# State-space output pass of a two-block model: products one step ahead, decays and outputs in two buffers, skip term on another engine

## What is computed

```python
decay = exp(where(lower, ac[..., :, None] - ac[..., None, :], -inf))       # ac: cumulated log decays of a chunk
y_intra = (einsum(cc, bc) * decay) @ xc                                      # within a chunk
y_inter = (cc * exp(ac)[..., None]) @ s_start                                # from the state at the chunk's start
y = y_f + flip_t(y_b) + d_skip[:, None] * xs                                 # both directions, and the skip term
y = y.reshape(b, T, SSD_DIM) * silu(z)
return rms_norm(y, norm_g)
```

## Time and profile before

| What | Value |
|---|---|
| Median of 3 runs | 3827.31 us (3821.52 to 3830.05) |
| The profiled execution's own time | 3822.47 us |
| Its span | 3820.6 us |
| Busy in the span: TensorE, VectorE, ScalarE, GpSimd | 3531.8, 2709.2, 869.0, 590.5 us |
| `ssd_stage` in it | 2789.6 to 2883.6 us |
| Granted TensorE clock, mean | 0.97 of full speed |

### The profile page before, as it was taken

One profiled execution on the slowest core, in us unless ns is written; L12 is line 12 of the kernel. 1 busy time (PEld: TensorE's weight loads), 2 busy tenths in 40 slices (PEclk: granted clock), 3 DMA queues, 4 the chain that ended last, 5 costly groups with the idle time before them and its releaser, 6 DMA issues. The chain is left out here.

```text
span 3820.6 us, 63639 instructions
## 1 busy us (share of the span) xinstructions
PE 3531.8 (92%) x25982; PEld 2197.3 (58%) x25982; DVE 2709.2 (71%) x3565; ACT 869.0 (23%) x1732; POOL 590.5 (15%) x579
## 2 busy tenths in 40 slices
PE   6999899988889999999999998999976998869995
PEld 2444488874355555555555555644555888435553
DVE  6889599995876676666666763787275778467773
ACT  2000022220122221212212211422235443012322
POOL 1112100004000000000000000321042875000110
PEclk9999999999999999999999999999998999979998
DMA  7674322225689999999999996312003000238996
GB/s 294 238 264 156 141 99 111 110 79 204 253 308 355 329 330 333 323 335 329 331 332 323 331 324 204 127 58 89 33 1 126 4 4 4 108 113 319 363 354 220
DMA packets 289274, 798.60 MB, mean 209 GB/s; under 512 B 18920, under 2 KB 25072, under 8 KB 274288
## 3 DMA queue, kind: packets, MB, share of 16 engines
q1 hardware_dynamic: 271152, 719.02, 51.7%
q0 software_dynamic: 17136, 73.54, 6.1%
q10 hardware_dynamic: 720, 2.17, 0.2%
HBM read 708.56 MB, written 86.11 MB: 208 GB/s over the span
## 5 line engine op out<-in xcount | busy, mean ns | idle before, releaser
L1706 PE MATMUL banks<-moe_down,moe_hidT 128*128 128x512 f32 x1280 | 565.5, 595 | 9.6 <-DMA moe_down<-d_wd 9.6
L1706 PEld LDWEIGHTS banks<-moe_down,moe_hidT 128*128 128x128 f32 x1280 | 237.8, 191 | 281.4 <-issue 276.5
L1779 ACT COPY moe_parts<-banks 128x512 f32<-128x512 f32 (+1 forms) x240 | 123.7, 516 | 852.6 <-PE banks L1685 849.6
L1685 PE MATMUL banks<-moe_wsums,moe_xsums 128*64 128x256 f32 x2560 | 302.0, 390 | 4.5 <-DVE moe_xsums L1823 2.5
L1685 PEld LDWEIGHTS banks<-moe_wsums,moe_xsums 128*64 128x64 f32 x2560 | 181.3, 140 | 131.3 <-issue 50.2
L1634 POOL DMA_INDIRECT moe_xe<-d_xhat,chosen x32 | 49.4, 1545 | 1132.7 <-PE banks L1678 1040.0
L913 PE MATMUL banks<-x_block,dft 128*128 128x256 f32 x896 | 197.3, 383 | 5.9 <-PEq L406 5.9
L913 PEld LDWEIGHTS banks<-x_block,dft 128*128 128x128 f32 x896 | 172.1, 192 | 30.2 <-issue 6.3
L1685 PE MATMUL banks<-x_block,moe_xeT 128*64 128x256 f32 x1536 | 182.1, 379 | 0.0
L1685 PE MATMUL banks<-x_block,moe_xsums 128*64 128x256 f32 x1536 | 182.1, 379 | 0.0
L1835 DVE TENSOR_TENSOR moe_wsums<-x_block 128x2048 f32<-128x2048 f32 x48 | 110.0, 2292 | 95.2 <-PE banks L1685 95.2
(11 more groups left out here) (512 smaller groups left out, 6729.9 us busy)
## 6 DMA issues: line engine op xcount, KB each, us to landing
moe_down<-d_wd SPq DMA_DIRECT2D x160, 1024.0 KB, 11.0
x_block<-d_wg SPq DMA_DIRECT2D x96, 1024.0 KB, 8.7
x_block<-d_wu SPq DMA_DIRECT2D x96, 1024.0 KB, 11.1
mix<-d_wg SPq DMA_DIRECT2D x64, 1024.0 KB, 8.6
mix<-d_wu SPq DMA_DIRECT2D x64, 1024.0 KB, 11.1
x_block<-d_seq SPq DMA_DIRECT2D x19, 1024.0 KB, 4.8
w_in_ring<-d_w_in SPq DMA_DIRECT2D x9, 2048.0 KB, 8.3
x_block<-d_mod_w SPq DMA_DIRECT2D x16, 1024.0 KB, 6.3
```

Of the source, the lines that this page charges most:

```text
L1685: last = nc.tensor.matmul(m.ps[out, bank, at], tokens(k), weights(kind * HK + k), start=(k == 0), stop=(k == HK - 1))
L1706: last = nc.tensor.matmul(m.ps[:, Y_BANK + h, :], hidT[:, j % 2, i * P:(i + 1) * P], wd[:, i, h * BANK:(h + 1) * BANK], start=(fc == 0 and ...
L1779: nc.scalar.copy(pp[:, to, :], m.ps[:, bank, 0:w * HN].rearrange("p (a n) -> p a n", a=w)).then_inc(s.copied, 1)
```

## The change

It does the following, in `ssd_stage` alone:

- TensorE: the Gram products, state products and first decays of chunk i + 1 (`front`) come ahead of the closing products of chunk i (`joined`); then the second decays of i + 1, and the transpose of the output of i - 2. The state products wait for `scaled` (the two readings of banks 4 and 5) in place of `y_read`. The closing products write banks 3 and 7 in turn.
- `decay` has two buffers per direction, by the parity of i. The Exp waits for the closing products of chunk i - 2.
- GpSimd makes the skip product into a new buffer of three, `y_skip`.
- VectorE: `scaled(i + 1)` (the two products out of PSUM and two adds) comes right behind the second `weighted` of i; then `normed(i - 2)`, then `joined(i - 1)`, which now begins with the add of the output bank.
- ScalarE: square root of chunk i - 2 behind the first Exp of i, copy of i - 3 behind the second.

```diff
--- before.py
+++ after.py
@@ -2625,13 +2625,14 @@
 
 def ssd_stage(nc, m, t):
 
-    s = signals(nc, "ssd", "lau xdt g_mm pair_mm e mm y_mm y_read yn tr_mm out gm int_mm var std vec")
+    s = signals(nc, "ssd", "lau xdt skip scaled g_mm pair_mm e mm y_mm y_read yn tr_mm out gm int_mm var std vec")
     with (
         nc.sbuf_tensor("decay_terms", [P, 2, SSD_H, P], F32) as lau,
         nc.sbuf_tensor("gram_masked", [P, 2, SSD_G, P], F32) as gm,
-        nc.sbuf_tensor("decay", [P, 2, SSD_H, P], F32) as seg,
+        nc.sbuf_tensor("decay", [P, 2, 2, SSD_H, P], F32) as seg,
         nc.sbuf_tensor("y", [P, 2, SSD_W], F32) as y,
         nc.sbuf_tensor("y_tmp", [P, 2, SSD_W], F32) as tmp,
+        nc.sbuf_tensor("y_skip", [P, 3, SSD_W], F32) as skip,
         nc.sbuf_tensor("y_mom", [P, 6], F32) as mom,
         nc.sbuf_tensor("y_mv", [P, 2, 2], F32) as mv,
         nc.sbuf_tensor("y_rstd", [P, 2], F32) as rstd,
@@ -2639,6 +2640,7 @@
     ):
 
         REACH, FROM = (0, 2), (1, 3)
+        Y = (3, 7)
         step_of = lambda d, i: 2 + (i if d == 0 else TT - 1 - i)
 
 
@@ -2651,10 +2653,19 @@
                                             t.dt[:, i, d * SSD_H:(d + 1) * SSD_H].unsqueeze(2).broadcast_to([P, SSD_H, HD]), ALU.mult
                                             ).then_inc(s.xdt, 1)
 
+            def skipped(i):
+                if i >= 3:
+                    pool.wait_ge(s.y_read, i - 2)
+                nc.gpsimd.tensor_tensor(skip[:, i % 3, :], t.xtm[:, i, :], t.rows[:, 0, :], ALU.mult).then_inc(s.skip, 1)
+
             for n in range(2 * TT):
                 i, d = n // 2, n % 2
+                if n == 2:
+                    skipped(0)
                 if n >= 2 and d == 0:
                     scaled_by_step(i - 1)
+                if n >= 3 and d == 1:
+                    skipped(i)
                 if n >= 2:
                     pool.wait_ge(s.pair_mm, n - 1)
                 nc.gpsimd.tensor_tensor(lau[:, d], t.tri[:, REACH[d], :].unsqueeze(1).broadcast_to([P, SSD_H, P]),
@@ -2682,8 +2693,7 @@
                                             lau[:, d, 3 * h:3 * h + 3, :].rearrange("p a b -> p (a b)"), start=True, stop=True)
                 last.then_inc(s.pair_mm, 1)
 
-            decays(0)
-            for i in range(TT):
+            def front(i):
                 at = slice(i * P, (i + 1) * P)
                 if i:
                     pe.wait_ge(s.gm, 2 * i)
@@ -2691,26 +2701,37 @@
                     last = nc.tensor.matmul(m.ps[:, 2, g * P:(g + 1) * P], t.chan[:, 3 + g, at], t.chan[:, 5 + g, at], start=True, stop=True)
                 last.then_inc(s.g_mm, 1)
                 if i:
-                    pe.wait_ge(s.y_read, i)
+                    pe.wait_ge(s.scaled, 2 * i)
                 for d in range(2):
                     for g in range(SSD_G):
                         w = SSD_W // SSD_G
                         last = nc.tensor.matmul(m.ps[:, 4 + d, g * w:(g + 1) * w], t.chan[:, 5 + g, at],
                                                 t.state[:, d, step_of(d, i), g * w:(g + 1) * w], start=True, stop=True)
                 last.then_inc(s.int_mm, 1)
-                decays(2 * i + 1)
-                pe.wait_ge(s.mm, 2 * i + 1)
-                if i + 1 < TT:
-                    decays(2 * i + 2)
+                decays(2 * i)
+
+            def joined(i):
+                if i >= 2:
+                    pe.wait_ge(s.y_read, i - 1)
                 pe.wait_ge(s.mm, 2 * i + 2)
                 pe.wait_ge(s.xdt, 2 * i + 2)
                 for h in range(SSD_H):
                     for d in range(2):
-                        last = nc.tensor.matmul(m.ps[:, 3, h * HD:(h + 1) * HD], seg[:, d, h, :], t.xdt[:, i, d, h * HD:(h + 1) * HD],
+                        last = nc.tensor.matmul(m.ps[:, Y[i % 2], h * HD:(h + 1) * HD], seg[:, i % 2, d, h, :], t.xdt[:, i, d, h * HD:(h + 1) * HD],
                                                 start=(d == 0), stop=(d == 1))
                 last.then_inc(s.y_mm, 1)
-                if i:
-                    turned(pe, i - 1)
+
+            front(0)
+            decays(1)
+            for i in range(TT):
+                if i + 1 < TT:
+                    front(i + 1)
+                joined(i)
+                if i + 1 < TT:
+                    decays(2 * i + 3)
+                if i >= 2:
+                    turned(pe, i - 2)
+            turned(pe, TT - 2)
             turned(pe, TT - 1)
 
         @block.scalar
@@ -2720,20 +2741,24 @@
                 nc.scalar.copy(m.mixT[:, POOL_T:POOL_T + 3, i * P:(i + 1) * P],
                                m.ps[:, 6, 0:SSD_W].rearrange("p (j c) -> p j c", c=P)).then_inc(s.out, 1)
 
+            def root(i):
+                act.wait_ge(s.var, i + 1)
+                nc.scalar.activation(rstd[:, i % 2:i % 2 + 1], rstd[:, i % 2:i % 2 + 1], ACT.Sqrt).then_inc(s.std, 1)
+
             for n in range(2 * TT):
                 i, d = n // 2, n % 2
                 act.wait_ge(s.pair_mm, n + 1)
-                if i:
-                    act.wait_ge(s.y_mm, i)
-                nc.scalar.activation(seg[:, d].rearrange("p (g h) i -> p g (h i)", g=2), m.ps[:, 0:2, 0:SSD_W], ACT.Exp).then_inc(s.e, 1)
-                if d == 0 and i:
-                    act.wait_ge(s.var, i)
-                    nc.scalar.activation(rstd[:, (i - 1) % 2:(i - 1) % 2 + 1], rstd[:, (i - 1) % 2:(i - 1) % 2 + 1], ACT.Sqrt).then_inc(s.std, 1)
-                if d == 1 and i:
-                    finish(i - 1)
-            j = (TT - 1) % 2
-            act.wait_ge(s.var, TT)
-            nc.scalar.activation(rstd[:, j:j + 1], rstd[:, j:j + 1], ACT.Sqrt).then_inc(s.std, 1)
+                if i >= 2:
+                    act.wait_ge(s.y_mm, i - 1)
+                nc.scalar.activation(seg[:, i % 2, d].rearrange("p (g h) i -> p g (h i)", g=2), m.ps[:, 0:2, 0:SSD_W], ACT.Exp).then_inc(s.e, 1)
+                if d == 0 and i >= 2:
+                    root(i - 2)
+                if d == 1 and i >= 3:
+                    finish(i - 3)
+            finish(TT - 3)
+            root(TT - 2)
+            finish(TT - 2)
+            root(TT - 1)
             finish(TT - 1)
 
         @block.vector
@@ -2752,25 +2777,27 @@
                 i, d = n // 2, n % 2
                 v.wait_ge(s.e, n + 1)
                 v.wait_ge(s.gm, n + 1)
-                sg = seg[:, d].rearrange("p (g h) i -> p g h i", g=SSD_G)
+                sg = seg[:, i % 2, d].rearrange("p (g h) i -> p g h i", g=SSD_G)
                 nc.vector.tensor_tensor(sg, sg, gm[:, d].unsqueeze(2).broadcast_to([P, SSD_G, SSD_H // SSD_G, P]), ALU.mult
                                         ).then_inc(s.mm, 1)
+
+            def scaled(i):
+                v.wait_ge(s.int_mm, i + 1)
+                for d in range(2):
+                    nc.vector.tensor_tensor(heads(tmp[:, d, :]), heads(m.ps[:, 4 + d, 0:SSD_W]),
+                                            wide_h(t.eac[:, i, d * SSD_H:(d + 1) * SSD_H]), ALU.mult).then_inc(s.scaled, 1)
+                v.wait_ge(s.skip, i + 1)
+                v.wait_ge(s.scaled, 2 * i + 2)
+                st.link(nc.vector.tensor_tensor(tmp[:, 0, :], tmp[:, 0, :], tmp[:, 1, :], ALU.add))
+                st.link(nc.vector.tensor_tensor(skip[:, i % 3, :], skip[:, i % 3, :], tmp[:, 0, :], ALU.add))
 
             def joined(i):
                 b = i % 2
                 yy = y[:, b, :]
-                v.wait_ge(s.int_mm, i + 1)
-                for d in range(2):
-                    st.did(nc.vector.tensor_tensor(heads(tmp[:, d, :]), heads(m.ps[:, 4 + d, 0:SSD_W]),
-                                                   wide_h(t.eac[:, i, d * SSD_H:(d + 1) * SSD_H]), ALU.mult))
-                st.wait()
-                st.link(nc.vector.tensor_tensor(tmp[:, 0, :], tmp[:, 0, :], tmp[:, 1, :], ALU.add))
-                st.link(nc.vector.tensor_tensor(tmp[:, 1, :], t.xtm[:, i, :], t.rows[:, 0, :], ALU.mult))
-                st.link(nc.vector.tensor_tensor(tmp[:, 0, :], tmp[:, 0, :], tmp[:, 1, :], ALU.add))
                 v.wait_ge(s.y_mm, i + 1)
                 if i >= 2:
                     v.wait_ge(s.tr_mm, i - 1)
-                nc.vector.tensor_tensor(yy, tmp[:, 0, :], m.ps[:, 3, 0:SSD_W], ALU.add).then_inc(s.y_read, 1)
+                nc.vector.tensor_tensor(yy, skip[:, i % 3, :], m.ps[:, Y[b], 0:SSD_W], ALU.add).then_inc(s.y_read, 1)
                 v.wait_ge(s.y_read, i + 1)
                 st.link(nc.vector.tensor_tensor(yy, yy, t.sz[:, i, :], ALU.mult))
                 st.link(nc.vector.bn_stats(mom[:], yy))
@@ -2789,10 +2816,17 @@
                 masked(2 * i)
                 weighted(2 * i)
                 masked(2 * i + 1)
+                if i == 0:
+                    scaled(0)
                 weighted(2 * i + 1)
+                if i + 1 < TT:
+                    scaled(i + 1)
+                if i >= 2:
+                    normed(i - 2)
                 if i:
-                    normed(i - 1)
```

(4 more changed lines are left out.)

## The result

The changed kernel is slower: 3838.4 us against 3825.2, medians of 11 executions each; the ratio is 1.0031, with a 95% interval from 1.0023 to 1.0039, so 8.8 to 14.9 us. One of its 11 executions took 10715 us; it is left out of the ratio, and nothing here explains it. The prediction had 3824.3, a gain of 3.0, and gave a chance of 0.10 to this side.

The account below looks back on a forecast made before the run. VectorE was taken to bound the stage. A gain of 5.7 us up to the fifteenth mask product, less 2.7 lost at the end, made 3.0 us less: 3824.3 us on the median, range 3815 to 3832.

Parts of the forecast that it names:

- new wait of E for the products: VectorE's two products out of PSUM wait for TensorE's state products: 0.6 us in an undisturbed step.
- The blocked add: One of VectorE's two adds in a step waits for GpSimd and takes about 1.5 us in place of 0.56.
- The lock with its hand-over of 0.15: GpSimd's hold on the shared port blocks VectorE, which goes on as if begun 0.15 us before GpSimd's end.
- a step without blocks: A step in the new order without any blocking by GpSimd: 9.27 us, against 9.22 in the kernel before.
- signs of being wrong: A step under 9.5 or over 11 us, no wait for the products, or a stage clock far from 0.93.
- The step laid out: Timeline of one new step: 10.36 us when settled, against 10.79 before; six steps 60.97 in sum.
- The skip product's price: GpSimd's multiply of 0.82 us lies under VectorE's statistics and costs it 0; VectorE loses 0.59 a step.
- case C: TensorE's clock falls in each of seven steps, 1.58 us each, 11.1 in all: 3835.4 us; chance 0.09.
- The end: From the last chunk's first mask product to the last copy: 14.5 us against 11.86, 2.7 lost.
- Case B: More blocking, by the skip multiply or a settled step staying at 10.79 us: 3827 to 3829 us; chance 0.18.
- A: GpSimd's second burst falls beside VectorE's adds: six steps 55.05 us instead of 60.97, whole 3818.4; chance 0.17.
- D: None of the waits or blocks binds; VectorE's work alone makes 8.0 us a step, whole 3811; chance 0.06.

Follow-up runs that it names:

- e9_before_skip: The kernel before with only the skip product moved to GpSimd, into three buffers; stage 96.8 us, ratio 1.0008.
- e2_one_input: The changed kernel with the variance operation given one tensor operand and two per-partition scalars; stage 102.9 us, ratio 1.0022.
- e11_warm_only8: The changed kernel with eight more matmuls a step on TensorE, results not read; stage 106.3 us, one execution.
- e8_warm_one_input: The changed kernel with eight more unread matmuls a step and the variance operation on one tensor operand; stage 99.3 us, one execution.
- e5_skip_vector: The changed kernel with the skip product back on VectorE, between the two adds; stage 106.0 us, ratio 1.0025.
- e4_scaled_last: The changed kernel with scaled(i + 1) moved behind joined(i - 1) in VectorE's order; stage 89.6 us, ratio 0.9988.
- e6_last_one_root: The changed kernel with scaled(i + 1) behind joined(i - 1), one-tensor variance, and the last but one chunk's root ahead of a copy; stage 87.7 us, ratio 0.9987.

## Why the prediction was wrong, point by point

**What held.** VectorE bounds the stage, and the wait for the Exp stays: 0.66 in four of the six steps. The new wait of E for the products is there in every step. The blocked add: 1.71 to 1.79 against "about 1.5" (by the layout some 1.8), though in three steps and not in each; in two others N is blocked instead, by 0.89. The skip product comes behind L2802 and under the statistics. The begin: third M 15.05 after GpSimd's first operation, predicted 15.4. The lock with its hand-over of 0.15 gave 0.67 where e9_before_skip measured 0.68. And a step without blocks, 9.27, carries the sum 11.65 above.

**What failed, by the steps of the prediction.** It laid six steps out at 60.97; the two profiles have 72.1 and 74.0. Of its own signs of being wrong two occurred: five steps are over 11, and the clock of the stage is 0.84.

1. *The step laid out.* It let GpSimd's first burst start 0.76 before the first M, which is in the middle of J, and counted "the small operations of J" as free of the port. One of them, the variance (L2805), reads two tensors from SBUF. Its list of operations with two SBUF operands (W, N, the two adds or the skip product) leaves this one out; in the kernel before no GpSimd operation ever fell on it, and it took 0.22 all eight times. It was blocked by 1.23 in four of the six steps, 4.9 us. e2_one_input shows the cause; e11_warm_only8 beside e8_warm_one_input gives the net price at full clock, 0.8 a step.

2. *The skip product's price.* It was taken as 0, for its own 0.82 only. What is queued behind it on GpSimd was not followed: L2671 could start once TensorE has used its terms, but stands behind the multiply, which waits for y_read, and so starts on L2805 (2823.25 and 2823.28). e5_skip_vector shows that this is not the whole of it: the block shrinks without the multiply, and does not go.

3. *The new wait, and the clock (case C).* E's wait was put at 0.2 in the settled step. It sums to 7.3 us over six steps. At full clock it is 0.5 to 0.9; the rest is the clock. Case C had the mechanism: idle time gathered ahead of front, and front on the path. It had about the price, 1.58: a step with a fall takes 13.13 or 13.33 where one without takes 11.65, and E's wait in the steps with a fall is 0.8 to 1.8 over the 0.49 of one without. But it argued against itself with TensorE's rising share of a step. The share did not rise, since the step got longer by the blocks, and the idle before front grew to 3.65 to 4.05 us in the steps with a fall, where 2.4 was laid out. The clock was at its lower level for a part of four of the six steps, of five in the second profile. The two costs were taken as separate cases; they come together, since a VectorE that is blocked lets TensorE idle. The blocked variance is not the only thing that does: in e2_one_input, without it, TensorE idles 2.4 to 3.4 before front and the clock falls in each of four steps.

4. *The end.* 14.5 predicted, 16.5 and 17.3 measured; in e4_scaled_last, at a clock of 0.84 there in place of 0.63, it takes 13.9. In the rows the products L2720 take 4.55 at a clock of 0.60, where 2.9 was taken from the kernel before:

```profile
2871.04 0.42 DVE L2773 TENSOR_TENSOR gram_masked<-banks,ssd_tri 128x256 f32<-128x256 f32 x1
...
2874.57 4.55 PE L2720 MATMUL banks<-hT,decay 128*128 128x64 f32 x24 [3.69 <-issue]
...
2880.30 1.28 ACT L2746 ACT_TABLE_LOAD   x1
...
2887.04 0.48 ACT L2741 COPY x_block<-banks 128x384 f32<-128x384 f32 x1 [1.85 <-PE banks L2681]
```

Sum: 4.9 and 5.8 (7.3 less some 1.5 for E's waits, which the layout has at 0.2 to 0.6 a step) are 10.7 of the 11.1 by which the six steps exceed the layout, the end adds 2.0 and the begin takes 0.4 off: 103.6 instead of 90.9. That says where the time stands in the rows, not what each cost alone would give back: without the blocked variance the waits for L2708 grew, and the stage fell by 0.7 to 3.4. Case B's settled step of 10.79, A and D did not occur.

**What stays open.** What decides on a fall of the clock. In the changed kernel it fell behind 3.65, 3.85 and 4.05 us of idling before L2701 and stayed behind 2.43 and 3.21; but in e2_one_input it fell behind 2.42, in e11_warm_only8 behind 2.27 (and stayed behind 1.88), and in the kernel before once behind 1.56, where it stayed behind 1.56 to 1.73 four times. The idle time ahead alone does not tell it. And whether two buffers alone make it fall more often.

## What to carry to other kernels

When a product is made ahead, look where its reader stands: here the maker was moved a step forward and the reader with it, with one operation between it and the one that lets the maker start, and the wait was made new; moving the reader back behind independent work (two lines) took 14 to 17 us off the stage. Where VectorE and GpSimd share a port, list every VectorE operation with two SBUF operands, the one-element ones too, and follow GpSimd's whole queue and not only the operation that is added; a block that is removed can reappear at the next such operation (0.43 of 0.54 in e6_last_one_root, 0.39 of 1.23 in e8_warm_one_input). A longer block of the bounding engine can cost again through the clock of the engine that idles meanwhile.

## What was not expected of the hardware

An operation of 128x1 elements on VectorE took 1.45 instead of 0.22 because a GpSimd multiply of 128x768 had begun 0.00 to 0.04 earlier; with its second operand given as a per-partition scalar, also from SBUF, it took 0.27 in every step. The Trainium skill (SBUF — State Buffer, "SBUF: two separate sides") names a VectorE operation with two SBUF inputs as one that takes the lock; the trace agrees for the smallest size, and shows for this operation that two per-partition scalars in SBUF do not count as such inputs. TensorE's granted clock was at its lower level for a part of four of six steps in the changed kernel, and stayed at 1.00 in the settled steps of e4_scaled_last and e6_last_one_root, with 2.4 us of idling before front in each; a fall made E wait 0.8 to 1.8 us longer.
